# Two transformer blocks in one launch: compression in rounded products, the second root from three sums, identity products in three pauses of TensorE

## The reference

```python
def first_block(x, ...):                  # per layer, one layer here
    h = rms_norm(x, attn_norm)
    x = x + hybrid_mixer(h, w_in, ...)    # 8 decay-gated heads; 8 heads over compressed and
                                          # windowed keys; @ w_out
    h = rms_norm(x, ffn_norm)
    x = x + (silu(h @ w_gate) * (h @ w_up)) @ w_down

def second_block(x, c, ...):
    sh1, sc1, g1, sh2, sc2, g2 = split(silu(c) @ ada_w + ada_b, 6)
    h = rms_norm(x, mix_pre_g) * (1 + sc1) + sh1
    y = hybrid_mixer(h, w_in, conv_w, ...)           # 8 heads and a causal convolution; @ w_out
    x = x + g1 * rms_norm(y, mix_post_g)
    h = rms_norm(x, ffn_pre_g) * (1 + sc2) + sh2     # its 1/rms is "the second root"
    y = (silu(h @ w_gate) * (h @ w_up)) @ w_down
    x = x + g2 * rms_norm(y, ffn_post_g)
```

## Time and profile before

| | us |
|---|---|
| median of three runs | 2262.01 (2261.34 to 2262.42) |
| the profiled execution, its own time | 2261.14 |
| its span | 2259.4 |
| TensorE busy | 2220.4 |
| VectorE busy | 1552.7 |
| ScalarE busy | 1086.9 |
| mean granted clock of TensorE over the span, in full speed | 0.996 |

### The profile page before, as it was taken

How to read it: one execution, slowest core, us unless ns; L and a number is a source line. 1 busy time by engine, 2 the same in 40 slices (tenths; PEclk the granted TensorE clock), 3 DMA queues, 4 the chain that set the end, 5 groups by cost and what they waited for, 6 DMA issues and landing times. The chain is left out here.

```text
span 2259.4 us, 29168 instructions
## 1 busy us (share of the span) xinstructions
PE 2220.4 (98%) x10164; PEld 1837.2 (81%) x10164; DVE 1552.7 (69%) x1990; ACT 1086.9 (48%) x1516; POOL 232.7 (10%) x216
## 2 busy tenths in 40 slices
PE   8999999999999999999999999989999999999998
PEld 7888877888888888888878887768888888888886
DVE  6455476877777778777866887977777444554456
ACT  5565463544444444344455776645444344434443
POOL 5003001000000000000001886000010000000000
PEclk9999999999999999999999999999999999999999
DMA  7656518798888888888856664867887666666664
GB/s 232 187 177 188 168 52 289 268 303 280 285 283 292 281 290 278 289 290 279 268 168 195 188 185 122 284 210 238 280 286 251 194 191 190 189 192 193 190 186 148
DMA packets 274500, 511.73 MB, mean 226 GB/s; under 512 B 20072, under 2 KB 28950, under 8 KB 274125
## 3 DMA queue, kind: packets, MB, share of 16 engines
q1 hardware_dynamic: 270252, 509.94, 71.3%
q10 hardware_dynamic: 4128, 0.26, 0.1%
HBM read 508.04 MB, written 2.10 MB: 226 GB/s over the span
## 5 line engine op out<-in xcount | busy, mean ns | idle before, releaser
L1909 DVE TENSOR_TENSOR w_lo<-raw,w_hi 128x1024 fp32r<-128x1024 f32 x760 | 944.1, 1246 | 539.8 <-ACT w_hi L1460 528.1
L1460 ACT ACTIVATE w_hi<-raw 128x1024 fp32r<-128x1024 f32 x760 | 802.4, 1060 | 952.1 <-PE bank L1025 892.4
L1041 PE MATMUL bank<-w_hi,act_hi 128*128 128x512 f32 x1984 | 776.0, 391 | 0.2 <-ACT w_hi L1460 0.2
L1042 PE MATMUL bank<-w_hi,act_lo 128*128 128x512 f32 x1984 | 772.3, 389 | 0.0
L1025 PE MATMUL bank<-w_lo,act_hi 128*128 128x512 f32 x2080 | 557.3, 390 | 0.0
L1025 PEld LDWEIGHTS bank<-w_lo,act_hi 128*128 128x128 f32 x2080 | 391.0, 188 | 82.6 <-DVE w_lo L1909 0.5
L1041 PEld LDWEIGHTS bank<-w_hi,act_hi 128*128 128x128 f32 x1984 | 372.5, 188 | 76.6 <-ACT w_hi L1460 0.6
L1042 PEld LDWEIGHTS bank<-w_hi,act_lo 128*128 128x128 f32 x1984 | 372.6, 188 | 76.0
L1041 PE MATMUL bank<-w_hi,mid_hi 128*128 128x512 f32 x960 | 376.0, 392 | 2.7 <-ACT w_hi L1460 2.0
L1042 PE MATMUL bank<-w_hi,mid_lo 128*128 128x512 f32 x960 | 373.7, 389 | 0.0
L1867 DVE SCALAR_TENSOR_TENSOR ada_acc<-ada_raw,c_act,ada_acc 128x512 f32<-128x512 f32 x360 | 269.8, 749 | 7.4 <-DMA ada_raw<-in_ada_w 0.4
(11 more groups left out here) (290 smaller groups left out, 1033.9 us busy)
## 6 DMA issues: line engine op xcount, KB each, us to landing
ada_raw<-in_ada_w SPq DMA_DIRECT2D x192, 512.0 KB, 5.1
raw<-in_w_gate SPq DMA_DIRECT2D x176, 512.0 KB, 4.5
raw<-in_w_up SPq DMA_DIRECT2D x176, 512.0 KB, 4.4
raw<-in_w_down SPq DMA_DIRECT2D x176, 512.0 KB, 4.5
raw<-in_w_in SPq DMA_DIRECT2D x168, 512.0 KB, 3.7
raw<-in_w_out SPq DMA_DIRECT2D x64, 512.0 KB, 5.4
raw<-in_cmp_w_k SPq DMA_DIRECT2D x4, 512.0 KB, 4.4
raw<-in_cmp_w_v SPq DMA_DIRECT2D x4, 512.0 KB, 4.5
```

The source lines that it names most:

```text
L1041: pe.matmul(A_[t][:, :], h_, w_hi[:, s, kk, :], start=(k == 0), stop=False)
L1042: pe.matmul(A_[t][:, :], l_, w_hi[:, s, kk, :], start=False, stop=False)
L1460: act.activation(w_hi[:, U % SPLIT_SLOTS].rearrange("p k n -> p (k n)"), raw[:, R % RAW_SLOTS].rearrange("p k n -> p (k n)"), ACT.Copy).th ...
L1909: dve.tensor_tensor(w_lo[:, U % SPLIT_SLOTS].rearrange("p k n -> p (k n)"), raw[:, R % RAW_SLOTS].rearrange("p k n -> p (k n)"), w_hi[:, U ...
```

## The change

It does three things.

1. *Compression in rounded products, tokens moving.* `blocks` holds the tokens with `pos` added, split into a rounded part and the rest, for both halves of the 32 positions. The eight `cmp_w` units are split like all other weights (`CMP`, eight units of `w_hi` and `w_lo`). For each l, a product with stationary `w_hi[l]` moves 64 columns (rounded and rest of 32 tokens), and one with `w_lo[l]` moves 32. The result has channels on partitions, so the keys' squares are summed with a product with ones, nothing is turned, and the values are spread by two transposes of `vrep`. The pieces lie at other steps of `attend`, and SyncE's special wait for these slots goes.
2. *The second root.* The mean of (x + r·y)² is formed from the sums of x² (there already), of x·y (`dot`, a new pass on VectorE with each y chunk) and of y² (`square(4, ...)` on ScalarE). `gated_add` is cut into four column quarters; the first stands in front of the root, the second behind the diagonal, the others inside the first chunk. At both roots `w_lo` of head units moves ahead of the last additions.
3. *Identity products.* `keep_busy(n)` multiplies the identity with itself n times into a bank that nobody reads then: 3 and 3 at the start, 13 at the first root, 20 at the second.

Its core:

```diff
+    pos["U"] += N_CMPU
+    CMP = [dict(R=R_CMP + 4 * kind, U=U_CMP + 4 * kind, C=None, nu=4, prev=None, ada=None, keep=None)
+           for kind in range(2)]
...
-        vcn = sb("vcn", [64, HD], F32, begin)
-        pick = sb("pick", [64, NSA_G, P], F32, begin)
-        filler("mid_fill", 4 * (KD * T - 2048 - 4 * TAB - 3 * P), begin)
-        blk_k = sb("blk_k", [P, CMP_BLOCK, 64], F32, begin)
-        blk_v = sb("blk_v", [P, CMP_BLOCK, 64], F32, begin)
+        vrep = sb("vrep", [P, NSA_G, P], F32, begin)
+        filler("mid_fill", 4 * (KD * T - 2048 - 4 * TAB - 2 * P), begin)
+        blocks = [sb(n, [P, 2, 2, NSA_G, T], F32R, begin) for n in ("blk_k", "blk_v")]
...
-                if R_CMP <= R < R_CMP + N_CMPU:
-                    sp.wait_ge(cmp_used, R - R_CMP + 1)
-                else:
-                    sp.wait_ge(lo_done, at((R if R < R_CMP else R - N_CMPU) + 1, r, stride))
+                sp.wait_ge(lo_done, at(R + 1, r, stride))
...
+            def keep_busy(n):
+
+                for _ in range(n):
+                    pe.matmul(TURN[1][:, 0:P], ident[:, :], ident[:, :], start=True, stop=True)
+
+            keep_busy(3)
...
                 turn_x(0)
+                keep_busy(3)
                 turn_x(1)
...
+                if n == 3:
+                    pe.wait_ge(x_new, TT * (KPU * u * P // CW + 1))
...
+                    keep_busy(13)
                     wait_read(pe, S_FFN1[-1]["C"])
                 else:
-                    pe.wait_ge(x_new, 2 * TT)
+                    keep_busy(20)
+                    pe.wait_ge(x_new, TT)
...
-                blk = (blk_k, blk_v)[kind]
-                pe.wait_ge(blk_zero, kind + 1)
-                pe.wait_ge(cum_copied, 1)
-                pe.wait_ge(blk_ready, 4 * (kind + 1))
                 for j in pieces:
-                    R = R_CMP + 4 * kind + j
-                    pe.wait_ge(raw_loaded[R % RAW_SLOTS], 16 * (R // RAW_SLOTS + 1))
-                    w = raw[:, R % RAW_SLOTS].rearrange("p a n -> p (a n)")
-                    for l in range(8):
-                        ins = pe.matmul(MISC[kind][0:64, 0:HD], blk[:, 8 * j + l, :], w[:, l * HD:(l + 1) * HD],
-                                        start=(j + l == 0), stop=(j == 3 and l == 7))
-                    ins.then_inc(cmp_used, 1)
+                    U = U_CMP + 4 * kind + j
+                    pe.wait_ge(hi_done, U + 1)
+                    pe.wait_ge(lo_done, U + 1)
+                    s = U % SPLIT_SLOTS
+                    for l_ in range(8):
+                        l = 8 * j + l_
+                        tok = blocks[kind][:, :, l // CMP_STRIDE, :, :].rearrange("p a g (n l) -> p a g n l",
+                                                                                  l=CMP_STRIDE)
+                        w_h = w_hi[:, s].rearrange("p a n -> p (a n)")[:, l_ * HD:(l_ + 1) * HD]
+                        w_l = w_lo[:, s].rearrange("p a n -> p (a n)")[:, l_ * HD:(l_ + 1) * HD]
+                        pe.matmul(MISC[kind][:, 0:64].rearrange("p (a g n) -> p a g n", a=2, g=NSA_G), w_h,
+                                  tok[:, :, :, :, l % CMP_STRIDE], start=(l == 0), stop=False)
+                        ins = pe.matmul(MISC[kind][:, 0:32].rearrange("p (g n) -> p g n", g=NSA_G), w_l,
+                                        tok[:, 0, :, :, l % CMP_STRIDE], start=False, stop=(l == CMP_BLOCK - 1))
+                    ins.then_inc(parts_used, 1)
...
                 if i == 2:
+                    compress(0, (3,))
...
+                    pe.wait_ge(kc_sq, 1)
+                    pe.matmul(MISC[0][:, 64:96], ones[:, :], kc_sum[:, 2, :], start=True, stop=True).then_inc(kc_summed, 1)
                     compress(1, (2, 3))
...
-            compress(0, range(4))
+            pe.wait_ge(cum_copied, 1)
+            pe.wait_ge(blk_lo, 4)
+            compress(0, range(3))
...
+                    if u == 5 and c in S_OUT2[1:]:
+                        wait_read(act, c["C"] - 1)
+                        q = c["prev"][2]
+                        for t in range(TT):
+                            square(4, t, q, y_acc[:, t, q * CW:(q + 1) * CW])
...
-                if i == 1:
+                if i == 0:
                     act.wait_ge(parts_used, LAST_U["in1"])
                     pre(LAST1, C_IN1, None)
-                    act.wait_ge(cmp_used, 4)
-                    link(act.activation(kcn[:, :], MISC[0][0:64, 0:HD], ACT.Square, accum_out=kc_ss[:, 0:1]))
-                    act.activation(kc_ss[:, 1:2], kc_ss[:, 0:1], ACT.Sqrt, bias=consts[0:64, 0:1],
+                    split(CMP[0], None, units=[3])
+                if i in (1, 2):
+                    split(CMP[1], None, units=[2 * i - 2, 2 * i - 1])
+                if i == 3:
+                    act.wait_ge(kc_summed, 1)
+                    act.activation(kc_rs[:, :], MISC[0][:, 64:96], ACT.Sqrt, bias=consts[:, 0:1],
                                    scale=1.0 / HD).then_inc(kc_std, 1)
...
-                for q in range(2):
-                    act.wait_ge(x_new, 2 * t + q + 1)
-                    square(4, t, q, x_res[:, t, q * D // 2:(q + 1) * D // 2])
+                if t == 0:
+                    act.wait_ge(y_copied, 1)
+                else:
+                    wait_read(act, LAST_C["out2"] - 1)
+                square(4, t, 3, y_acc[:, t, D - CW:D])
...
+            def dot(t, q):
+
+                cols_q = slice(q * CW, (q + 1) * CW)
+                dve.tensor_tensor_reduce(zsb[:, 0, :], y_acc[:, t, cols_q], x_res[:, t, cols_q], 1.0, 0.0, ALU.mult,
+                                         ALU.add, x_dot_y[:, t, q:q + 1]).then_inc(dot_done, 1)
+                dve.wait_ge(dot_done, TT * q + t + 1)
...
                 ins.then_inc(diag_made, 1)
+                if n == 3:
+                    gated_add(1)
                 scale(0)
                 low(0)
-                if n == 2:
-                    split(c, None, units=[1])
...
+                    if n == 3 and u in (2, 4):
+                        gated_add(u // 2 + 1)
...
+                if u == 0:
+                    dve.wait_ge(turn_out_a, n)
+                    dve.wait_ge(turn_out_d, n)
+                if 2 <= u < 6:
+                    kind, ab = u % 2, u // 2 - 1
+                    dve.wait_ge(blk_hi, u - 1)
+                    dve.tensor_tensor(blocks[kind][:, 1, ab, :, :].rearrange("p g t -> p (g t)"), full_of(kind),
+                                      blocks[kind][:, 0, ab, :, :].bitcast(F32).rearrange("p g t -> p (g t)"),
+                                      ALU.subtract).then_inc(blk_lo, 1)
+                    dve.wait_ge(blk_lo, u - 1)
+                if u < 4:
+                    kind, ab = u % 2, u // 2
+                    n_b = T // CMP_STRIDE - ab
+                    pc = pos_cols[:, kind * CMP_BLOCK + CMP_STRIDE * ab:kind * CMP_BLOCK + CMP_STRIDE * (ab + 1)]
+                    src = heads[("kc", "vc")[kind]][:, :, CMP_STRIDE * ab:]
+                    dve.tensor_tensor(full_of(kind).rearrange("p (g t) -> p g t", g=NSA_G)[:, :, 0:T - CMP_STRIDE * ab].rearrange(
+                                          "p g (n l) -> p g n l", l=CMP_STRIDE),
+                                      src.rearrange("p g (n l) -> p g n l", l=CMP_STRIDE),
+                                      pc.unsqueeze(1).unsqueeze(1).to_broadcast([P, NSA_G, n_b, CMP_STRIDE]),
+                                      ALU.add).then_inc(blk_add, 1)
...
+                    if how == "gated_copy":
+                        wait_read(dve, C - 1)
+                        for t in range(TT):
+                            dot(t, n)
...
+                if i == 0:
+                    split(CMP[0], None, units=[3])
                 if i == 2:
+                    dve.wait_ge(parts_used, U_CMP + 4)
+                    link(dve.tensor_copy(kc_sum[:, 0, :], MISC[0][:, 0:32]))
+                    link(dve.tensor_tensor(kc_sum[:, 1, :], MISC[0][:, 32:64], kc_sum[:, 0, :], ALU.add))
+                    dve.tensor_tensor(kc_sum[:, 2, :], kc_sum[:, 1, :], kc_sum[:, 1, :], ALU.mult).then_inc(kc_sq, 1)
+                if i in (1, 2):
+                    split(CMP[1], None, units=[2 * i - 2, 2 * i - 1])
+                if i == 4:
                     dve.wait_ge(kc_std, 1)
-                    link(dve.reciprocal(kc_ss[:, 2:3], kc_ss[:, 1:2]))
-                    dve.tensor_scalar(kcn[:, :], MISC[0][0:64, 0:HD], kc_ss[:, 2:3], None, ALU.mult).then_inc(kc_n, 1)
...
+            split(S_IN2[0], None, units=range(2))
             for t in range(TT):
                 last_add(LAST_FFN1, LAST_C["ffn1"], t)
-            split(S_IN2[0], None, units=[0])
...
-            for t in range(TT):
-                last_add(LAST_OUT2, LAST_C["out2"], t)
-            mean_root(3)
-            gated_add()
             split(S_FFN2[0], None, units=[EARLY_HEAD - 1])
-            mean_root(4)
+            last_add(LAST_OUT2, LAST_C["out2"], 0)
+            dot(0, 3)
```

(22 more changed lines are left out.)

103 lines of the change are left out of this document (51 added, 52 removed).

## The result

The changed kernel is slower: 2269.43 us median of 11 runs (2264.29 to 2271.77), the kernel before 2262.42 us beside it (11 runs, 2261.21 to 2264.06). The ratio is 1.0027, 95% interval 1.0019 to 1.0035. The forecast was 2256, in a range of 2252.5 to 2262; the time lies at the place of rival (1). The profiled execution took 2269.43 us, with a span of 2267.7 us.

A forecast was written before the change was run, and what follows sets the result against it. TensorE, busy 98% of the span, was taken as the bound, through its work, idling and clock. Start -0.9, second root -4.0, first root -1.3 and compression +0.4 summed to -5.8, so 2256 us, range 2252.5 to 2262.

The forecast's parts named there:

- rival (1): Compression: the clock falls to 0.50 between 270 and 290, small records take twice as long, +14 to 2270; chance 0.14.
- the compression term: Compression: records at 0.107 to 0.117 us, saved work lost to waiting, vcmp's copy moved into a wait; +0.4 us.
- The start: First weights products: identity products bring full clock sooner; -0.9 us, bounds 0 and 1.1 gained.
- The first root: Pause before S_IN2: thirteen identity products keep full clock, moved w_lo brings the mean sooner; -1.3 us.
- The second root: Pause before S_FFN2: shorter chain -3.0, clock kept up -1.4, adds moved into the first chunk +0.4; -4.0 us.
- The chain: Second root, from y through dots, reciprocal and two adds to the diagonal: TensorE starts 3.0 us sooner.
- the gated adds in the first chunk: Six adds moved behind the second root into S_FFN2's first chunk: +0.4 us, bounds 0 and +2.5.
- rival (2): The three pauses: the fill doesn't hold the clock; 2257.2 at the second root alone, 2259.3 at all three; chance 0.18.

The follow-up runs named there:

- evenly wide kernel: The changed kernel with both small compression products of a pair moving the same 64 token columns twice, 128 columns a record: 2257.83 us, ratio 0.9980.
- fourfold one: The changed kernel with each small compression product moving its token columns four times, 256 or 128 columns a record: 2264.13 us, ratio 1.0013.

## Why the prediction was wrong

**The step that failed** is the compression term, at +0.4. Its working priced a record by the row nearest to it, L1184 in the earlier trace rows, and with the pitch it took over the full clock at which that row ran, for 1.9 us. The stage measured +11.85 up to the ninth job and +0.3 behind it. The pitch was right (0.111 against 0.107 to 0.117). The clock was not: with 64 and 32 columns moved behind each load of 128 columns it fell at 273.5, with the end of the third piece, and came back at 300.9, among attention's work. This is rival (1) as it was written, and the window it named (0.50 between 270 and 290) decides. What the experiments add is a series: in the profiled executions the same loads at the same pitch with more columns behind them lose the clock later (128 and 64) or not at all (128 and 128). The share that PE is busy, 10.00 of 10 in all of them, does not show it.

**Its size.** Rival (1) had +14, every small record at twice its time. Measured are +11.85 in the profile and +11.4 by the kernel with compression alone. Of the 128 records 48 had run before the fall; the 80 others cost 0.10 more each, 8.2 together. The other 3.6 are about what the transposes, scores and products of attention cost that ran at half clock between and behind them. That its 2270 is so close to 2269.43 is partly luck, because the pause ahead of S_FFN1 put 2.8 on top in the profiled execution.

**The chance.** 0.14 for it was too low. The argument for it was made from a row (20 of 107 ns), the one against it (dense transposes and scores between the pieces) from none. From 285.5 to 289.1 such work ran between two pieces, and the clock stayed at 0.50. The Trainium skill ("TensorE: Matmul & The Clock Gate", "What's actually happening") says that the clock follows how busy TensorE has been. The trace does not agree where busy is read as the profile's busy share, which was 10.00 of 10 at a clock of 0.50 and 10.00 of 10 at 1.00 with more columns moved.

**The start**, -0.9: -0.7. The four products at 8.18 take 1.20 us, as named. The size has little weight, since the arrival of x moves the marker, and six identity products do not always bring the clock up in time: the four products take 2.06 us in the evenly wide kernel's profile and 1.66 in the fourfold one's. In the profiles with six products it stands at 11.25 to 11.74 in seven of eight (13.39 in one), in the four without at 12.18 to 13.45.

**The first root**, -1.3: -1.35, right in mechanism and size. What is avoided is the fall of the clock, and that fall is not certain: without the fill the stretch from the diagonal to the row sums took 6.28, 5.16, 7.31 and 6.15 us in four profiles, with the thirteen products 5.15 to 5.17 in all eight.

**The second root**, -4.0: -4.4 in the profile. The chain gave 3.7 instead of 3.0. Four rows of VectorE, the dots and what closes the chain:

```profile
1518.48 0.69 DVE L1645 CUSTOM_DVE_ANT_0 zsb<-y_acc,x_res 128x512 f32<-128x512 f32 x1
...
1520.10 0.67 DVE L1645 CUSTOM_DVE_ANT_0 zsb<-y_acc,x_res 128x512 f32<-128x512 f32 x1
...
1522.27 1.41 DVE L2092 SCALAR_TENSOR_TENSOR x_res<-y_acc,rstd,x_res 128x512 f32<-128x512 f32 x2
...
1523.59 0.16 DVE L2248 RECIPROCAL rstd<-std 128x2 f32<-128x2 f32 x1
```

The second dot ends at 1520.8, 3.3 us after the start of the last products, where the working had 3.8: it took 0.76 us and a gap for each dot, while a dot took 0.67 to 0.69 and neighbours in VectorE's queue overlap by up to 0.1 us. The clock gave 1.36 where 1.4 was said, and the gated adds in the first chunk cost 0.6 instead of 0.4:

```profile
1543.72 1.21 PE L1041 MATMUL bank<-w_hi,act_hi 128*128 128x512 f32 x4 [0.32 <-ACT act_hi L1310]
```

That a rest of 2.5 us might bring the clock down was rival (2), with 0.18. The rest was 1.85 us, and over the profiles with twenty products behind the new root the clock fell in two of six. So the rival holds in part: the fill does not hold the clock each time. In those two the stretch took 6.22 and 6.28 us, 1.1 more than in the others, where the rival had 1.2 (and the sum 1.4 for the same fall).

**Left out** was the wait for `act_lo` ahead of S_FFN1. Its 0.9 us in the profile before looked fixed. It was 0.8 in one other profile and 1.3 to 2.1 in the other ten, since ScalarE's splits there wait for transfers, and in two of them the clock fell behind it. The profile of before was at the good end. The two short waits are those of the two kernels with neither identity products nor new compression, so the change may make the wait longer; profiles of one or two executions of each kernel don't show it.

## What to carry to other kernels

A busy TensorE is not a fast one. When products get narrower, look at the granted clock over that stretch and not at the busy share, and price as a rival that it stands at half clock, for all that stands near them too. Padding the moving side to 128 columns cost 0.002 us a record here and kept the clock in both profiles, with a doubt left by some longer runs. A fill pays when it closes a pause, so shorten the pause first, and look at what the engines behind it must now deliver sooner; price the two together.

## What the runs showed of the hardware

- A stream of rounded products with 128 columns of weights and 64 or 32 moved ran at 0.111 us a record at full clock and 0.213 at half; 128 moved columns cost hardly more (0.113), and 256 of them took 0.22.
- The clock fell to 1.2 GHz while TensorE had no gap at all (at 273.5 in the changed kernel), and it can come and go within the stage: in the kernel with compression alone it was back at 1.00 from 292 to 294 and at 0.60 in the window behind.
- Whether a given gap costs the clock changes from one execution to the next: the same 1.85 us did in two profiles and not in four, the 2.1 us for `act_lo` did in one profile of the changed kernel and the 1.8 us in the next did not. One profile is one draw; the ranges of the runs (7.5 us for the changed kernel, 2.9 for the one before beside it) show it.
